# Pass order inside a product, a third operand split ahead, and GLA states moved in halves, in a one-core hybrid decoder layer

## The reference, cut to what matters

```
h     = rmsnorm(x)
proj  = h @ w_in                       # gates ga, gb; conv inputs B, C, x, g; q, k, v, g; rank-16 code
za    = B * conv3(C * x) * silu(g)     # branch a input
S_t   = diag(alpha_t) S_{t-1} + k_t^T v_t ;  o_t = q_t S_t      # GLA, 4 heads, state 256 x 512 per head
zb    = rmsnorm_head(o) * silu(g)      # branch b input
x    += (sigmoid(ga) * (za @ w_branch_a) + sigmoid(gb) * (zb @ w_branch_b)) @ w_out
y     = rmsnorm(x)
```

## Time and profile before

| what | value |
|---|---|
| timed runs | 2553.20, 2555.18, 2558.56 us (median 2555.18) |
| profiled execution: device time, span | 2554.59 us, 2552.8 us |
| busy share: PE, DVE, ACT, GpSimd | 98%, 70%, 42%, 8% |
| mean granted clock of TensorE | 0.989 |
| heads and gates, until | 779 us |
| pairs 0 to 51, phase A, phase B, output | 779 to 1943, to 2122, to 2308, to 2552.8 us |

### The profile page before, as it was taken

How to read it: one execution, slowest core, us unless ns; L and a number is a source line. 1 busy time by engine, 2 the same in 40 slices (tenths; PEclk the granted TensorE clock), 3 DMA queues, 4 the chain that set the end, 5 groups by cost and what they waited for, 6 DMA issues and landing times.

```text
span 2552.8 us, 44375 instructions
## 1 busy us (share of the span) xinstructions
PE 2494.6 (98%) x18552; PEld 2455.0 (96%) x18552; DVE 1788.5 (70%) x2528; ACT 1066.6 (42%) x1556; POOL 195.5 (8%) x309
## 2 busy tenths in 40 slices
PE   7999999999999999999999999999999999999995
PEld 7999999999989999999999999999999999999995
DVE  6458657585678878787787888876668778774322
ACT  5343444433444434443443444444455444334332
POOL 2001001010110000000000011100000110110000
PEclk9999999999999999999999999999999999999997
DMA  6225335153344434334443445654669669457221
GB/s 196 77 57 165 102 88 178 52 174 101 111 159 112 116 100 110 103 90 113 116 116 100 109 124 162 176 144 125 190 184 292 209 209 292 141 168 225 68 81 74
DMA packets 443099, 351.44 MB, mean 138 GB/s; under 512 B 12868, under 2 KB 415728, under 8 KB 438928
## 3 DMA queue, kind: packets, MB, share of 16 engines
q1 hardware_dynamic: 412560, 231.69, 33.0%
q0 software_dynamic: 30352, 117.09, 13.8%
HBM read 278.24 MB, written 70.50 MB: 137 GB/s over the span
## 4 chain that ended last, share of the span: by engine, by line
PE 90%; DMA 4%; DVE 3%; ACT 1%; issue 1%; SPq 0%; ACTq 0%; POOL 0%; DVEq 0%
PE bank L1507 32%; PE acc L1507 25%; PE acc L1432 18%; PE acc L412 6%; PE acc L1336 2%; PE acc L1400 1%; PE bank L1364 1%; DMA raw<-in_w_out 1%; PE bank L1397 1%; DMA raw<-in_w_in 1%; DMA ma_d<-mix_tile 1%; PE bank L1394 1%; DMA x_f<-zt_d 1%; PE bank L1368 0%; DVE act_x L2182 0%
## 5 line engine op out<-in xcount | busy, mean ns | idle before, releaser
L1626 DVE TENSOR_TENSOR ring_lo<-pa,ring_hi 128x1024 fp32r<-128x1024 f32 x476 | 581.5, 1222 | 191.1 <-ACT ring_hi L884 188.0
L884 ACT ACTIVATE ring_hi<-pa 128x1024 fp32r<-128x1024 f32 x476 | 502.6, 1056 | 367.1 <-PE bank L1507 209.9
L1432 PE MATMUL acc<-act_y,w_hi 128*128 128x288 f32 x2560 | 520.7, 299 | 0.6 <-DVE w_lo L388 0.6
L1432 PEld LDWEIGHTS acc<-act_y,w_hi 128*128 128x128 f32 x2560 | 412.8, 190 | 3.9 <-issue 2.2
L1432 PE MATMUL acc<-act_y,w_lo 128*128 128x288 f32 x1280 | 378.9, 296 | 0.0
L1507 PE MATMUL bank<-act_x,ring_hi 128*128 128x288 f32 x2240 | 338.8, 296 | 0.6 <-ACT act_x L1172 0.4
L1507 PE MATMUL bank<-act_y,ring_hi 128*128 128x288 f32 x2112 | 321.7, 295 | 1.8 <-ACT act_y L1172 1.6
L1507 PEld LDWEIGHTS bank<-act_x,ring_hi 128*128 128x128 f32 x2240 | 312.0, 188 | 1.0 <-ACT act_x L1172 0.6
L1507 PE MATMUL acc<-act_x,ring_hi 128*128 128x288 f32 x1984 | 301.1, 296 | 0.0
L1507 PEld LDWEIGHTS bank<-act_y,ring_hi 128*128 128x128 f32 x2112 | 294.0, 189 | 2.5 <-ACT act_y L1172 1.8
L1507 PEld LDWEIGHTS acc<-act_x,ring_hi 128*128 128x128 f32 x1984 | 277.3, 189 | 0.0
(11 more groups left out here) (314 smaller groups left out, 3166.8 us busy)
## 6 DMA issues: line engine op xcount, KB each, us to landing
pa<-in_w_in SPq DMA_DIRECT2D x208, 512.0 KB, 5.2
raw<-in_w_in SPq DMA_DIRECT2D x40, 1024.0 KB, 5.8
states<-in_state_gla POOLq DMA_DIRECT2D x32, 512.0 KB, 4.4
out<-states POOLq DMA_DIRECT2D x32, 512.0 KB, 3.8
pa<-in_w_branch_a SPq DMA_DIRECT2D x32, 512.0 KB, 6.3
pa<-in_w_branch_b SPq DMA_DIRECT2D x32, 512.0 KB, 4.7
raw<-in_w_out SPq DMA_DIRECT2D x16, 1024.0 KB, 6.0
gate_tile<-gate_d POOLq DMA_DIRECT2D x32, 288.0 KB, 3.5
```

The source lines that it names most:

```text
L884: A(ring_hi[g % RING][:, :], piece_of[src][u % 2][:, :], ACT.Copy).then_inc(part_hi, 1)
L1432: mm = nc.tensor.matmul(half_bank[h % 2][:, 0:HALF], (w_hi, w_lo)[a][par][:, k * P:(k + 1) * P], y_of(k, b, j), start=(k == 0 and n == 0), ...
L1626: V.tensor_tensor(ring_lo[g % RING][:, :], piece_of[SOURCE[p]][u % 2][:, :], ring_hi[g % RING][:, :].bitcast(F32), ALU.subtract).then_inc( ...
```

## The change

Three edits. First, in all pairs but 0, 52 and 60 the PE loop waits for `part_lo` before the product's first matmul and runs the passes innermost, in the order `PASSES` (hi x hi, hi x lo, lo x hi). Second, in phase A the operand of product 5 of phase B ("s4 b22") joins products 4 and 6 in `AHEAD`; the three rounds of load, split and store are moved, by new keys in `SPLITS` and new places in the GpSimd queue. Phase A's own operands keep their places. Third, states are loaded and stored as two halves of 256 KB, each half with a store semaphore of its own, and each half's store waits only for its own update.

```diff
-AHEAD = (4, 6)
-SPLITS = {-35: 4, -21: 6, -4: 0, 4: 1, 6: 2, 8: 3, 10: 5}
+AHEAD = ((4, 6), (4, 6, 5))
+SPLITS = ({-35: 4, -21: 6, -4: 0, 4: 1, 6: 2, 8: 3, 10: 5},
+          {-38: 4, -30: 6, -23: 5, -4: 0, 4: 1, 6: 2, 8: 3})
...
             def load_state(i, j):
-                if NS * i + j >= 2:
-                    pool.wait_ge(st_out[j % 2], 8 * NS * i + 16 * (j // 2))
-                pool.dma_start(states[:, j % 2, :, :], state_gla[0, j, i, :, :].rearrange("(k p) v -> p k v", p=P)
-                               ).then_inc(st_in[j % 2], 16)
+                rows = state_gla[0, j, i, :, :].rearrange("(k p) v -> k p v", p=P)
+                for kk in range(KK):
+                    if NS * i + j >= 2:
+                        pool.wait_ge(st_out[j % 2][kk], 8 * NS * i + 16 * (j // 2))
+                    pool.dma_start(states[:, j % 2, kk, :], rows[kk]).then_inc(st_in[j % 2], 16)
...
-                    pool.wait_ge(seq_upd, i * NS + j + 1)
-                    pool.dma_start(new_gla_sample[0, j, i, :, :].rearrange("(k p) v -> p k v", p=P),
-                                   states[:, j % 2, :, :]).then_inc(st_out[j % 2], 16)
+                    rows = new_gla_sample[0, j, i, :, :].rearrange("(k p) v -> k p v", p=P)
+                    for kk in range(KK):
+                        pool.wait_ge(seq_upd, (i * NS + j) * KK + kk + 1)
+                        pool.dma_start(rows[kk], states[:, j % 2, kk, :]).then_inc(st_out[j % 2][kk], 16)
...
                 if m == 0:
                     pool.wait_ge(prod_done, NPROD * PAIR_A)
                     load_ahead(1, 0)
-                if m == 2:
-                    store_ahead(1, 0)
-                    load_ahead(1, 1)
-                if m == 4:
-                    store_ahead(1, 1)
+                if m in (1, 2):
+                    store_ahead(1, m - 1)
+                    load_ahead(1, m)
+                if m == 3:
+                    store_ahead(1, 2)
...
-                    for n, (a, b) in enumerate(((0, 0), (1, 0), (0, 1))):
-                        if n == 1:
+                    late = u in (0, PAIR_A, PAIR_B)
+                    if not late:
+                        pe.wait_ge(part_lo, g + 1)
+                    order = [(n, k) for n in range(3) for k in range(KH)]
+                    if not late:
+                        order = [(n, k) for k in range(KH) for n in range(3)]
+                    for n, k in order:
+                        a, b = ((0, 0), (1, 0), (0, 1))[n] if late else PASSES[n]
+                        if late and k == 0 and n == 1:
                             pe.wait_ge(part_lo, g + 1)
-                        if n == 2 and fresh:
+                        if late and k == 0 and n == 2 and fresh:
                             pe.wait_ge(x_lo, fresh)
```

More of the change, by code:

```diff
@@ L300, in hybrid_kernel @@
         st_in = [sem(f"st_in{n}") for n in range(2)]
-        st_out = [sem(f"st_out{n}") for n in range(2)]
+        st_out = [[sem(f"st_out{n}{k}") for k in range(2)] for n in range(2)]
         inter_saved, chunk_mm, chunk_sq, chunk_state, sp_out = (
@@ L421, in slot_of, with aheads, split_count @@
             return (y_f32 if f32 else act_y)[:, kh * KH:(kh + 1) * KH, b, j * HALF:(j + 1) * HALF]
+        def aheads(f):
+            return sum(len(AHEAD[n]) for n in range(f + 1))
+        def split_count(f, p):
+            return 4 + NPROD * f + list(SPLITS[f].values()).index(p) + 1
         def phase_of(u):
@@ L524, in load_operand @@
                 slot = SLOTS[f + 1][p]
[L525 removed]
+                if p in AHEAD[f]:
                     for b in range(2):
[L527 removed]
+                        sp.dma_start(slot_of(slot, b).bitcast(F32), zs_d[f, AHEAD[f].index(p), b]).then_inc(blk_in[p], 16)
                 else:
@@ L659, in _ @@
             pool.dma_start(gate_d[0, GATE_UNITS - 1], mix_tile[:, 1, :]).then_inc(extra_out, 16)
-            pool.wait_ge(st_out[0], 16 * (NS // 2) * H)
-            pool.wait_ge(st_out[1], 16 * (NS // 2) * H)
+            for n in range(2):
+                for kk in range(KK):
+                    pool.wait_ge(st_out[n][kk], 16 * (NS // 2) * H)
             pool.wait_ge(sp_out, 16 * H)
@@ L1164, in _ @@
                     for h, start in ((1, PAIR_A), (2, PAIR_B)):
-                        q = SPLITS.get(g - (start - 1) * NPROD)
+                        q = SPLITS[h - 1].get(g - (start - 1) * NPROD)
                         if q is not None:
-                            slot = SLOTS[h][0 if q in AHEAD else q]
-                            if q in AHEAD:
-                                act.wait_ge(ahead_in, 16 * (len(AHEAD) * (h - 1) + AHEAD.index(q) + 1))
+                            slot = SLOTS[h][0 if q in AHEAD[h - 1] else q]
+                            if q in AHEAD[h - 1]:
+                                act.wait_ge(ahead_in, 16 * (aheads(h - 2) + AHEAD[h - 1].index(q) + 1))
                             else:
-                                act.wait_ge(blk_in[q], 16 * h)
+                                act.wait_ge(blk_in[q], 16 * (h + sum(q in AHEAD[n] for n in range(h - 1))))
                             A(slot_of(slot, 0), slot_of(slot, 1, True), ACT.Copy).then_inc(x_hi, 1)
@@ L1482, in _ @@
                         fresh = (1, 2, 4, 6).index(p) + 1
-                    if u in (PAIR_A, PAIR_B) and p in AHEAD:
-                        pe.wait_ge(blk_in[p], 32 * f)
+                    if u in (PAIR_A, PAIR_B) and p in AHEAD[f - 1]:
+                        pe.wait_ge(blk_in[p], 16 * (f + sum(p in AHEAD[n] for n in range(f))))
                     elif u in (PAIR_A, PAIR_B):
-                        fresh = 4 + NPROD_SPLIT * (f - 1) + SPLIT_ORDER.index(p) + 1
+                        fresh = split_count(f - 1, p)
                     if fresh:
@@ L1928, in _ @@
                     for r in range(2):
-                        dve.wait_ge(st_out[r], 16 * (NS // 2) * H)
+                        for kk in range(KK):
+                            dve.wait_ge(st_out[r][kk], 16 * (NS // 2) * H)
                     dve.wait_ge(o_ready, NCH * H)
```

44 lines of the change are left out of this document (20 added, 24 removed).

## The result

The changed kernel takes 2564.43 us (median of 10 runs, 2556.34 to 2567.71) and the kernel before, run beside it on the same chip, 2553.23 us (10 runs, 2549.70 to 2558.56). The ratio is 1.0036, with a 95% interval of [1.0024, 1.0048]: slower by 0.36%, some 9 us. (The means of the two sets differ by 9.3 us, their medians by 11.2; the ratio goes with the means.) The forecast was 2567 in 2554 to 2578, slower.

The account below looks back on a forecast made before the run. PE, busy 98% of the span, was taken to bound the kernel. The terms 0 + 0.9 + 4.1 + 4.5 + 3.2 + 0.8 + 1.6 - 3.1 = +12.0 us on 2554.6 gave 2566.6, forecast as 2567, range 2554 to 2578.

Parts of the forecast that it names:

- early wait at pair 53: Start of pair 53, where DVE is behind: PE waits for `ring_lo` before the first matmul, +0.9 us.
- stall at (55, 1): Phase A: the first load ahead lands late, delaying ACT, DVE's `ring_lo` and then PE, +4.1 us.
- stall at (56, 1): Phase A: the second store and load, issued later, make `ring_lo` late for PE again, +4.5 us.
- clock behind them: Phase A: one drop to half clock after each of two gaps over 4 us, 1.6 us per drop, +3.2 us.
- start of phase B, with one more drop: Products 5, 6 and (61, 0): PE waits for added transfers, +0.8 us, plus one more clock drop, +1.6 us.
- 1, the pace: Changed pairs: the pass order leaves PE's 132.9 ns per matmul unchanged, 0 with up to 3 us either way.
- The third rival: Changed pairs: the pass order shifts PE's pace; at one nanosecond per matmul, 11 us, total 2556; chance 0.04.
- 2, the wait in front: Product starts: the early `ring_lo` wait costs only where it is late; +0.9 us at pair 53.
- 3, the rounds: Phase A: store-to-landing chains of 17.3 us, now one pair apart, stall PE twice, +4.1 and +4.5 us.
- the loads ahead land in time: Phase A: the round ends within 13.0 us, so stalls and their clock drops vanish; sum +0.2, total 2555; chance 0.10.
- 4, the start of phase B: Products 5, 6 and (61, 0): the added transfer costs 4.2 us; +0.8 us net, +1.6 for a clock drop.
- 5, the states: Last states in the heads: halves shorten the store and load chain, so PE's 2.9 us wait goes, -3.1 us.

Follow-up runs that it names:

- e4_pass_states: Kernel before with the new pass order, its early wait and the states in halves, without the third operand ahead: 2546.01 us, ratio 0.9969.
- e8_late_pairs: Kernel before with new pass order and states in halves, no third operand ahead, pairs 53 and 61 also keeping the old order and later wait: 2542.26 us, ratio 0.9956.
- e6_rows_lohi: Kernel before with wait in front and row blocks outermost, but inner order hi x hi, lo x hi, hi x lo: 2546.44 us, one run.
- e7_wait_front: Kernel before with only the wait for `ring_lo` moved to the front, passes still outermost: 2556.07 us, one run.
- e5_late_rounds: Changed kernel with the splits of operands 6 and 5 moved later, to (55, 0) and (56, 3): 2544.70 us, ratio 0.9971 of the kernel before.
- e3_ahead: Kernel before with only the third operand ahead and its moved rounds: 2565.89 us, ratio 1.0049.
- e11_two_rounds: Kernel before with its two rounds one pair apart, operand 5 still split in phase B: 2558.38 us, one run.
- e9_k_order: Kernel before with the row blocks of each pass taken as 0, 4, 1, 5, 2, 6, 3, 7, passes outermost: 2551.79 us, one run.
- e1_pass: Kernel before with only the new pass order and the early wait for `ring_lo`: 2547.19 us, ratio 0.9981.

## Why the prediction was right

The direction, the place and the order of what happens were as it said, and they did not hang on luck: without the gain in pace the changed kernel would be some 16 us slower than before (9.3 + 6.8, an estimate from the table), which is still in the range. That the size came so near was luck in part: the pace, the one term that was missed, took off 6.8 us and the start of phase B 1.3, and the gaps, their clock and the smaller gain of the states put 4.1 to 5.5 us back.

| term of the sum | predicted | measured in the trace |
|---|---|---|
| pace of the pairs | 0 (3 either way) | -5.5 in pairs 0 to 51, -0.6 in the rest of B, some -0.7 in A |
| early wait at pair 53 | +0.9 | +0.9 (A of e4_pass_states less that of e8_late_pairs, 180.4 - 179.5) |
| stall at (55, 1) | +4.1 | +5.0 |
| stall at (56, 1) | +4.5 | +5.4 |
| clock behind them | +3.2 | +4.4 to 5.5 |
| start of phase B, with one more drop | +2.4 | +1.1 |
| states | -3.1 | -2.0 in the changed kernel, -2.5 over all kernels (see 5) |

**1, the pace: the step that failed.** It read "The trace has both orders side by side, the head stage in the new one, and they differ by 0.3 ns", and took a bound of 3 us from it. The head stage has other moving operands, and the pace goes with the operand's slot: in pairs 2 to 49 of the kernel before products differ from 131.96 to 133.33 ns, more than the orders do. Two stages with different operands could therefore neither show a gain nor bound one. Measured on the same operands it is 132.94 to 132.31 ns, 0.63 ns, some 6.9 us over the 10,920 matmuls that change; the table's -5.5, -0.6 and -0.7 are these. The third rival had this mechanism, at 1.0 ns and a chance of 0.04; its mechanism came true beside the stalls and not in place of them. What the prediction said of the weight loads held: the changed kernel has as many weight loads as matmuls, 18552 (the page's first part), and e6_rows_lohi has the full gain with no neighbours that share weights.

```profile
PE 2487.4 (97%) x18552; PEld 2447.7 (96%) x18552; DVE 1787.4 (70%) x2528; ACT 1066.1 (42%) x1556; POOL 220.8 (9%) x376
```

**2, the wait in front.** Right at pair 53. At (61, 0) the prediction had it too, but only together with the added transfer; alone it takes the wait from 2.11 to 3.6 us there (e7_wait_front).

**3, the rounds.** The chain was right link by link. The first store was to be issued 1993.0 - (2010.87 - 22.33) = 4.5 us into pair 54 and was, at 4.4. From store to load 10.55 us passed (9.92 predicted), the load took 7.67 (7.4). The first gap is 0.9 us longer than predicted, as these two terms add up. The second round was slower, 11.5 us from store to load and 8.84 us to land, 3.1 us over the forecast; its gap is still only 0.9 us longer, since PE, at half the clock behind the first gap, came to (56, 1) 2.3 us later. That the rival "the loads ahead land in time" could not come true, and with it the rule of the Trainium skill ("DMA: Bandwidth & Descriptors", "Anatomy of one DMA — SWDGE (gpsimd) path"), shows in the same rows: by the rule a load of 1152 KB takes some 4.7 us (an estimate from the page), the trace has 7.67 and 8.84. e5_late_rounds shows the mechanism from the other side: with two and three products more between the splits PE does not wait at (55, 1) and (56, 1).

**The clock.** "This is the price of one drop" was taken from a gap of 2.11 us with 3.4 us at half the clock. The gaps of 5.0 and 5.4 us brought stretches of some 6.8 us each, twice as long, the first part of which fell into the gap itself. The price of a drop was mis-sized, 2.2 to 2.7 us instead of 1.6. Their number, two, was right here, but e3_ahead had one drop for two gaps and e11_two_rounds none for one, so that it could have come out otherwise.

**4, the start of phase B.** Gaps of 2.6, 1.55 and 0.8 us at products 5, 6 and (61, 0), predicted 3.7, 2.5 and 0.8: the places and releasers are right, and the added transfer cost about one us less than the 4.2 taken for it, between the two ends given. The extra drop did not come in this profile; in others of the set the same stretch has 0, 3.4 or 6.8 us at half the clock.

**5, the states.** The direction was right, the working was not. It said that store and load of the later half take about 7.5 us instead of 10.7, and that PE's wait goes. In the chain from the store's issue at 713.26 to the load's landing at 724.86 they took 11.6 us, no less than before, and 1.4 us of the wait stayed (1.1 to 1.8 in the other five kernels with halves). What the trace does show is an earlier start, as the store begins after one update of 0.76 us and not after two of 1.42 together. The gain is clear of the clock drops once the start of the heads is taken off as well. From the first head matmul to the first pair, less half of the time at half the clock between them (an estimate), the seven kernels without halves take 726.5 to 727.6 us, mean 726.9, and the six with them 723.9 to 724.7, mean 724.4: 2.5 us less (before 726.7, the changed kernel 724.7; the 1.75 us of the result count its heads' later start by 0.2 us against it). The forecast was 3.1.

## What to carry to other kernels

A chain of store, landing and reload through one slot has a length of its own, here 18 to 20 us and 5 more for the split, and what has to be checked is the distance of its consumers, not the bandwidth: splits 7 or 8 products apart (22 to 26 us) stalled PE, splits 10 apart did not. A wait that is moved in front of more work costs nothing where its producer is ahead, but it adds what it used to hide (here 8 matmuls, 1.06 us) to every stall that some other edit brings, so that two edits of one diff are to be costed together. Where a matmul is run ten thousand times, no other stage's pace stands for it: 0.6 ns were 7 us here, and only the same operands in both orders tell.

## What the runs showed of the hardware

The pace of a matmul of 128 x 288 at the full clock went with the slot of the moving operand (131.7 to 132.0 ns for y11 and y21, 133.3 for y12, y22 and the slots of `act_x`) and with the order of the matmuls, 0.63 ns less on average with row blocks outermost; weights or a moving tile in common between neighbours had no part in it. What in the slot does it stays open.

The clock did not follow the length of a gap alone. Gaps of 5.0 and 5.4 us brought 6.8 us at half the clock each, one of 2.11 us in the kernel before 3.4 us. The gap of 3.4 us at (55, 1) brought 6.8 us in e3_ahead and none in e11_two_rounds; the 2.6 and 3.0 us of e5_late_rounds brought none. PE's wait at the last states, 2.8 to 3.0 us in seven kernels, had 3.4 us at half the clock right behind it in four of them (e3_ahead, e6_rows_lohi, e7_wait_front, e9_k_order) and none in three (before, e1_pass, e11_two_rounds). And in the heads of all kernels but the changed one the profile has 3.4 to 20.5 us at half the clock, in stretches that differ from one execution to the next of nearly the same work. Those of 6.8 us (at 277, 432 to 438 and 587 to 592 us) have no gap of PE over 0.5 us in the 30 us before them. By half of their length they move a run by up to 10 us (an estimate). The runs of one kernel lie 7 to 12 us apart, and the longer ones have the lower mean clock: of 17 runs of the kernel before, the shortest (2549.40 us) had 0.992 and the longest (2557.90) 0.988, and in every series of six or more the two go together (correlation -0.87 to -0.99). Where in those runs the clock was low only a profile would show. So a profile must be read by its stages before its total is.
